# VectorE takes each step of the mLSTM's gates behind the maximum and rotation of its attention tile, in a two-layer hybrid encoder step

## What is computed

```python
# attention of the prompt, per head and block of 128 queries
s = einsum(q, k) * MLA_SCALE ; s = where(mask, s, -big)
p = softmax(s) ; o = p @ v
# gates of the mLSTM: 4 heads x 640 tokens, which no step of the attention reads
li = ml_i + gb[0] ; lf = log_sigmoid(ml_f + gb[1])
b = cumsum(lf)
m_t = maximum(b + m, running max of (li - b) + b)
w_inter = exp(b + m - m_t) ; exp(-m_t) ; w_s = exp(b_last - b + li - m_new)
```

## Time and profile before

| | before |
|---|---|
| median of 3 executions | 2612.91 us (2611.38 to 2613.08) |
| the profiled execution | 2612.57 us, of which the span from first to last instruction is 2610.8 us |
| TensorE busy | 2567.4 us, 98% |
| VectorE busy | 1643.0 us, 63% |
| ScalarE busy | 1136.1 us, 44% |
| GpSimd busy | 532.5 us, 20% |
| TensorE's mean granted clock | 0.997 |

### The profile page before, as it was taken

One profiled execution on the slowest core, in us unless ns is written; L12 is line 12 of the kernel. 1 busy time (PEld: TensorE's weight loads), 2 busy tenths in 40 slices (PEclk: granted clock), 3 DMA queues, 4 the chain that ended last, 5 costly groups with the idle time before them and its releaser, 6 DMA issues.

```text
span 2610.8 us, 44639 instructions
## 1 busy us (share of the span) xinstructions
PE 2567.4 (98%) x17903; PEld 2455.3 (94%) x17903; DVE 1643.0 (63%) x2563; ACT 1136.1 (44%) x1919; POOL 532.5 (20%) x440
## 2 busy tenths in 40 slices
PE   8999999999999999999999999999999999999998
PEld 8999999996689999999999999999956899999998
DVE  5665575646466766657587574765564757757573
ACT  5343344424654534334454342553165535434253
POOL 0010112103754101011210110121066441101011
PEclk9999999999999999999999999999999999999999
DMA  3322324220025132232313222334101161322321
GB/s 113 93 81 81 88 74 113 74 59 11 20 54 100 38 93 81 81 97 66 113 33 94 85 71 75 89 89 105 27 11 34 42 130 33 97 81 71 91 79 59
DMA packets 369747, 190.73 MB, mean 73 GB/s; under 512 B 38494, under 2 KB 365489, under 8 KB 369583
## 3 DMA queue, kind: packets, MB, share of 16 engines
q1 hardware_dynamic: 365582, 178.03, 25.4%
q0 software_dynamic: 4000, 10.47, 1.7%
HBM read 182.53 MB, written 5.93 MB: 72 GB/s over the span
## 4 chain that ended last, share of the span: by engine, by line
PE 95%; DVE 2%; ACT 1%; issue 1%; DMA 0%; SPq 0%; DVEq 0%; another core or an unknown queue 0%; ACTq 0%
PE ps L728 27%; PE ps L729 27%; PE ps L730 27%; PE ps L1092 2%; PE ps L1103 1%; PE ps L1135 1%; PE ps L1154 1%; PE ps L1144 1%; PE ps L1204 1%; PE ps L1205 1%; DVE at L2669 0%; PE ps L1226 0%; PE ps L1217 0%; PE ps L1316 0%; PE ps L1366 0%
## 5 line engine op out<-in xcount | busy, mean ns | idle before, releaser
L728 PE MATMUL ps<-xh,w 128*128 128x320 f32 x1920 | 595.9, 310 | 3.4 <-DVE css L2931 3.4
L730 PE MATMUL ps<-xh,w 128*128 128x320 f32 x1920 | 593.9, 309 | 0.0
L729 PE MATMUL ps<-xl,w 128*128 128x320 f32 x1920 | 593.9, 309 | 0.0
L1526 ACT ACTIVATE w<-raw 128x512 fp32r<-128x512 f32 (+3 forms) x372 | 315.9, 861 | 486.3 <-PE ps L730 466.2
L3028 POOL TENSOR_TENSOR hl<-ub,hh 128x640 fp32r<-128x640 f32 x88 | 174.2, 1980 | 1451.0 <-ACT hh L1526 1383.8
L728 PE MATMUL ps<-hh,w 128*128 128x320 f32 x1408 | 438.0, 311 | 3.3 <-DVE ub L2325 1.2
L730 PE MATMUL ps<-hh,w 128*128 128x320 f32 x1408 | 435.0, 309 | 0.0
L729 PE MATMUL ps<-hl,w 128*128 128x320 f32 x1408 | 435.0, 309 | 0.0
L728 PEld LDWEIGHTS ps<-xh,w 128*128 128x128 f32 x1920 | 360.9, 188 | 5.6 <-DVE css L2931 3.9
L729 PEld LDWEIGHTS ps<-xl,w 128*128 128x128 f32 x1920 | 361.1, 188 | 0.3
L730 PEld LDWEIGHTS ps<-xh,w 128*128 128x128 f32 x1920 | 360.9, 188 | 0.0
(11 more groups left out here) (415 smaller groups left out, 4680.0 us busy)
## 6 DMA issues: line engine op xcount, KB each, us to landing
raw<-in_w_ffn_in_dram SPq DMA_DIRECT2D x176, 512.0 KB
raw<-in_w_ffn_out_dram SPq DMA_DIRECT2D x192, 192.0 KB
raw<-in_w_in_dram SPq DMA_DIRECT2D x38, 512.0 KB
raw<-in_w_ffn_out_dram SPq DMA_DIRECT2D x64, 128.0 KB
wraw<-in_w_out_dram SPq DMA_DIRECT2D x8, 512.0 KB
raw<-in_w_out_dram SPq DMA_DIRECT2D x8, 512.0 KB
out_dram<-xio SPq DMA_DIRECT2D x5, 512.0 KB
xin<-in_x_prompt_dram SPq DMA_DIRECT2D x1, 2048.0 KB, 8.2
```

The costliest lines, as they stand in the source:

```text
L728: pe.matmul(out, wh, xh, start=first, stop=False, skip_group_check=loose)
L729: pe.matmul(out, wh, xl, start=False, stop=False, skip_group_check=loose)
L730: return pe.matmul(out, wl, xh, start=False, stop=last, skip_group_check=loose)
L1526: return nc.scalar.activation(out, in_, func, **kw)
```

## The change

In VectorE's loop over the tiles, the block of `maximum(n)`, the two calls of `rotated`, `inverse_sums` and `pair_output` is moved up, ahead of the steps of the gates. Each gate step now stands behind the block of its own n. `scaled` in steps 4 and 6 still stands first. Nothing is added or removed, and TensorE, ScalarE, GpSimd and SyncE keep their lists.

```diff
             for n in range(NT):
                 if n in (4, 6):
                     scaled(l, n // 2 - 2)
+                if n % PT_ == PT_ - 1 and n // PT_ + 1 < H:
+                    rotated(n // PT_ + 1, 1)
+                maximum(n)
+                if n % PT_ == 0 and n // PT_ + 1 < H:
+                    rotated(n // PT_ + 1, 0)
+                if n % 8 == 1 and n > 8:
+                    inverse_sums(n // 8 - 1)
+                if n % 8 == 4 and n > 8:
+                    pair_output(n // 8 - 1)
                 if n == 5:
                     gate_magnitude()
...
                 if n == 16:
                     gate_negative()
-                if n % PT_ == PT_ - 1 and n // PT_ + 1 < H:
-                    rotated(n // PT_ + 1, 1)
-                maximum(n)
-                if n % PT_ == 0 and n // PT_ + 1 < H:
-                    rotated(n // PT_ + 1, 0)
-                if n % 8 == 1 and n > 8:
-                    inverse_sums(n // 8 - 1)
-                if n % 8 == 4 and n > 8:
-                    pair_output(n // 8 - 1)
```

## The result

The changed kernel takes 2618.07 us (median of 20 executions, 2615.26 to 2621.74) against 2612.18 us for the kernel before in the same comparison (20 executions, 2609.04 to 2613.43). The ratio is 1.0026, with a 95% interval of 1.0020 to 1.0032: slower, by a quarter of a per cent. The forecast of 2614.7 us was too low and its range ended at 2617.0. The prediction called a time above 2618.1 slower and gave that 4%; the measured time lies at this edge.

A forecast was written before the change was run, and what follows sets the result against it. TensorE was taken as the bound, waiting in the attention only at a 0.72 us gap ahead of tile 13. Terms 0.62 + 0.36 = 0.98 us a layer, 1.96 in both, gave 2614.7 us; range 2611.5 to 2617.0.

The forecast's parts named there:

- What bounds the kernel: TensorE, busy 98% of the span; in this stretch its one idle gap is 0.72 us ahead of tile 13's transposes.
- the exponential of 14: Sign of being right: at tile 14 ScalarE's exponential waits less for its maximum than 1.18 us.
- the gap at 13: Sign of being right: TensorE's gap ahead of the transposes of tile 13 remains, at 0.7 to 1.1 us.
- scores 12 were released by the rotation: Sign of being wrong: scores 12 or 16 released by VectorE's `qt` after a gap of over 0.5 us.
- Tile 11, +0.62: Sources ahead of `rotated(3, 1)` wait for a GpSimd addition and become 2.01 us; transposes of 11 come 0.62 us later.
- The sign that line 2692 would end with the addition: Sign of being right: line 2692's first scan or copy takes about 1.4 us, not 0.76, ending with a GpSimd addition.
- Tile 13, +0.36: Behind the first pair's output the scan (1.64 us) replaces the ends (1.28); tile 13's exponential is 0.36 us later.
- the first rival: Nothing in the way: GpSimd's additions fall elsewhere, sources cost 1.40 us; 0.45 us a layer, 2613.7 us; 21%.
- Tiles 14 and 15, 0: Tile 14's 0.74 us gain closes no TensorE gap; at 15 line 2716 takes 0.87 us, leaving scores 16 in time.
- The fourth: Rotations become the bound, both meeting whole GpSimd additions, and a new head's scores wait: 2619.7 us; 4%.
- The third: Every overlap blocks: VectorE also waits for GpSimd's single-operand products, line 2716 at tile 15; 1.5 us a layer, 2615.8; 11%.
- My rule from line 2721: VectorE instructions with two inputs run unhindered inside GpSimd's single-operand products: line 2721 took 670 ns inside one.

The follow-up runs named there:

- after_no_adds: The changed kernel with GpSimd's additions of the convolution's taps replaced by a one-element fill: 2610.89 us, ratio 1.0001 to the kernel before.
- scan_first: The changed kernel with the scan of the maxima taken ahead of the pair's output: 2613.67 us, ratio 1.0011 to the kernel before.
- behind_from_12: The kernel before with only gate steps 12 to 16 moved behind the maximum, 5 to 11 staying ahead: 2611.65 us, ratio 1.0002 to the kernel before.
- after_filled: The changed kernel with eight unread TensorE products ahead of the transposes of tile 13: 2614.82 us, ratio 1.0016 to the kernel before.
- behind_to_11: The kernel before with only gate steps 5 to 11 moved behind the maximum, 12 to 16 staying ahead: 2617.52 us, ratio 1.0028 to the kernel before.
- max_13_early: The changed kernel with maximum 13 taken ahead of the pair's output and so ahead of the scan: 2621.86 us, ratio 1.0043 to the kernel before.
- behind_from_13: The kernel before with only gate steps 13 to 16 moved behind the maximum, the scan staying ahead of maximum 12: 2609.40 us, ratio 0.9996.

## Why the prediction was wrong

**What bounds the kernel** held: TensorE's gap ahead of tile 13 was the place, and both layers behaved alike. Of the signs that the prediction named, the exponential of 14 waited 0.43 us in place of 1.18, as foretold; the gap at 13, foretold at 0.7 to 1.1 us, was 2.21; and scores 12 were released by the rotation behind a gap of over 0.5 us, which had been named as a sign of being wrong.

**Tile 11, +0.62.** It came out at +0.75. The sources met the addition as I had it from the first copy of the starts. The first of them took 1.24 us, 0.48 more than before, where I had 0.61 more; the second, the copy, was lengthened as well, from 0.60 to 0.86 us, beside the product that followed. Mechanism right, size nearly, and that partly because these two errors balance. The sign that line 2692 would end with the addition was misread from the start: by my own sum it waits for the addition and then takes its 0.76 us, and it did end 0.68 us behind it.

**Tile 13, +0.36. This is the step that failed first.** I priced the scan at the 1.55 us that it had taken in the earlier trace rows, and its exchange for the ends at 1.64 - 1.28. The term measured 1.54 us. Of this, 1.14 is the scan's own lengthening, from 1.55 to 2.69: an addition had begun 0.20 us before it. The 0.36 of the exchange itself was right (`after_no_adds`, gap 0.99 against 0.65). One paragraph earlier I had shown from the earlier trace rows that such an instruction waits for an addition under way, and applied it to the sources alone. I didn't ask the same of the next moved step, although I let it start at a new time. Under the first rival I wrote of the addition at tile 11 that it can hardly come earlier, and it didn't; but the one at tile 13 came 0.90 us earlier, since VectorE's moved steps no longer held GpSimd up. `scan_first` shows the term with the order turned round, `after_no_adds` without the addition, and `behind_from_12` with the scan 0.15 us ahead of the addition; all three give a gap of 0.5 to 1.0 us.

**The clock, no term at all, is the other.** I wrote that TensorE stood waiting for 0.72 us and took each further microsecond of waiting as one microsecond. At a gap of 2.2 us the granted clock went to its lower level behind it, and that cost 1.66 us more in each layer. `after_filled` takes it back (1.54), and the two layers of `behind_to_11` show it alone (1.71). No row of before has TensorE waiting so long within the attention, but the trace of before did show the price elsewhere, at the start of the first layer's output projection. TensorE had stood idle for 1.84 us, and 1 us later the granted clock fell (a row of TensorE, then a window whose 0.57 is the clock):

```profile
808.16 0.42 PE L728 MATMUL ps<-xh,w 128*128 128x320 f32 x1 [1.84 <-DVE css L2931]
```
```profile
809.00:813.00 4.00, 4.00 (x19) 4.00 (x18) 4.00 (x6) 1.19 (x2) 4.00 (x4) 0.57 0.94 262
```

A mean of 0.57 over 4 us is some 3.4 us at half the clock, which costs 1.7 us by estimate. A TensorE gap that might grow to 1.8 us or more should have carried this as a possible term in each layer.

**Tiles 14 and 15, 0.** Right for this kernel, but by luck: line 2716 took 1.89 us, not the 0.87 that I chose, because an addition of 660.60 stood where I had put a product, and it was hidden only because TensorE was so late already; in `max_13_early` the same step, 3.15 us long, cost a gap of 1.74 us.

**The rivals.** The fourth, rotations as the bound, gave nearly the right total (2619.7, with 4%) for another reason. Its mechanism was seen at scores 12 (0.99 us of gap, in place of 0.52) and in `max_13_early` in full (1.74 us at scores 16), yet it carried only 0.75 of the 3.9 us. The third, in which every overlap blocks, isn't borne out as a whole, but not refuted either. Line 2708 started at 659.24 in the changed kernel, inside GpSimd's product of 657.29 to 659.90, and took its usual 0.81 us, and line 2721 of before is a second such case. Yet where a VectorE instruction began 0.16 to 0.24 us behind the start of a product over 128 x 512, it took longer: the ends' exponents 1.27 us in place of 0.87 (`max_13_early`), the scan 1.78 in place of 1.47 (`behind_to_11`); and a copy of 3 elements 0.58 in place of 0.14 (`after_no_adds`). My rule from line 2721, that a single-operand product never holds such an instruction up, was too wide; these waits are 0.3 to 0.4 us where the additions cost up to 1.2, and no run takes the products away. So of the Trainium skill's page "SBUF — State Buffer", section "SBUF: two separate sides", the part that matters for the loss, that whoever starts first keeps the other out, is what `scan_first` and `behind_from_12` show for VectorE's scan against GpSimd's product and addition. The part that the other is kept out for the whole instruction is not what the rows show for GpSimd's single-operand products.

**The total.** 0.75 + 1.54 + 1.66 = 3.95 us a layer, 7.8 measured in both, against 5.9 between the medians and about 6.8 by the ratio. Between the two profiled executions it is 6.1, and there the difference can be followed: after starts 1.0 us later, loses 7.8 in the attention, and gets back 1.4 in the output projection of the first layer and 1.5 near the end (0.2 stay elsewhere). The 1.4 is the clock's fall of before shown above; at the same place after has a gap of 1.69 us and keeps 1.00. Near the end before has the lower clock for some 7 us and after for 3.4. So what seemed missing is the clock in other places, which differs from one execution to the next. Whether it accounts for the medians too isn't shown, nor why after starts 1.0 us later.

By its own words the range was a little narrow as well: rival 3's 2615.8 with the spread of 1.7 on top is 2617.5, not 2617.0. The measured time lies outside both.

## What to carry to other kernels

When a step is moved on an engine, give it a new duration, not the one that it had: look at what the other engines will be doing at its new time, and ask it of every moved step, not of the first. The other engines' times change with it: a step that leaves lets them run earlier, here by 0.9 us. The wait that a step causes counts by who starts first, so a few tenths of a microsecond decide whether a scan costs 1.5 or 2.7 us. And a gap on TensorE that grows from under one to over two microseconds may cost more than its length, since the clock can fall behind it; the trace of before, read over its whole span and not only in the stage at hand, can already hold the price. Either the work is moved where the gap doesn't grow, or the gap is filled.

## What the runs showed of the hardware

- A VectorE scan of 4 x 640 elements took 1.43 to 1.55 us with no GpSimd addition under way at its start (with two exceptions: 1.65 inside the end of another two-input GpSimd instruction, 1.78 when it began 0.24 us behind a product) and 2.69 us when a GpSimd addition over 128 x 640 had begun 0.20 us before. A VectorE copy of 3 elements took 0.14 to 0.16 us when nothing held it, 1.38 us behind such an addition and 0.58 when it ended with a product. Turned round, a GpSimd addition of 1.54 us took 2.65 and a product of 0.60 us took 1.62 behind a scan.
- A GpSimd product with one operand let VectorE instructions with two run unhindered when they began 0.6 us or more behind its start (line 2708 of the changed kernel, line 2721 of before, line 2716 of `behind_from_13`), and cost them 0.3 to 0.4 us when they began 0.16 to 0.24 us behind the start of one over 128 x 512. No run was made to separate this.
- The granted clock of TensorE fell to its lower level (0.50, 1.2 GHz) in both layers behind a gap of 2.2 us; in two of three places behind a gap of 1.84 us (before at 808, and one of two layers of `behind_to_11`); in one of two behind gaps of 1.29 and 1.74 us one behind the other (`max_13_early`); and in none behind single gaps of 0.5 to 1.7 us in the attention and the output projection. With the gap of 2.2 us filled to 0.46 us by products without use it stayed at 2.4 GHz. Each of these falls lasted over 3 us and cost 1.3 to 1.7 us.
